# A two-layer encoder on one core: the third branch's attention weights turned by DVE blocks and DRAM transfers in place of TensorE

## The reference, cut to what matters

```python
s = jnp.where(valid, s, -1e30)
lse = jax.nn.logsumexp(s, axis=-1)
o = einsum('bhrnql,bhrnld->bhrnqd', exp(s - lse[..., None]), vb)      # per pattern
...
wts = jax.nn.softmax(jnp.stack(lses, axis=0), axis=0)
o_c = jnp.einsum('gbhs,bhsd->bhsd', wts, outs)
```

## Time and profile before

| | us |
|---|---|
| median of three runs | 1249.8 (1249.55 to 1250.07) |
| the profiled execution's own time | 1250.1 |
| its span, first to last instruction | 1248.1 |
| TensorE busy | 1221.4 (98%) |
| GpSimd busy | 838.0 (67%) |
| DVE busy | 676.7 (54%) |
| ScalarE busy | 433.6 (35%) |
| mean granted TensorE clock, as a share of full speed | 0.997 |

### The profile page before, as it was taken

How to read it: one execution, slowest core, us unless ns; L and a number is a source line. 1 busy time by engine, 2 the same in 40 slices (tenths; PEclk the granted TensorE clock), 3 DMA queues, 4 the chain that set the end, 5 groups by cost and what they waited for, 6 DMA issues and landing times.

```text
span 1248.1 us, 17785 instructions
## 1 busy us (share of the span) xinstructions
PE 1221.4 (98%) x5840; PEld 983.5 (79%) x5840; DVE 676.7 (54%) x1008; ACT 433.6 (35%) x775; POOL 838.0 (67%) x595
## 2 busy tenths in 40 slices
PE   6999999999999999999999999999999999999995
PEld 4887788778878887788888878887887788777884
DVE  5675327522843374677557831573257335738842
ACT  5424423442354245200253453245314532450002
POOL 5597367737763876678849853885498549757871
PEclk9999999999999999999999999999999999999998
DMA  6243223323332333374234332523252315336621
GB/s 240 72 131 121 102 86 117 112 93 101 109 103 93 109 101 118 126 269 151 90 137 143 102 104 77 162 83 107 70 155 87 117 50 151 101 103 228 207 68 67
DMA packets 51794, 148.64 MB, mean 119 GB/s; under 512 B 6560, under 2 KB 8096, under 8 KB 51360
## 3 DMA queue, kind: packets, MB, share of 16 engines
q1 hardware_dynamic: 28800, 103.04, 24.5%
q10 hardware_dynamic: 22944, 44.98, 11.8%
HBM read 114.45 MB, written 16.78 MB: 105 GB/s over the span
## 4 chain that ended last, share of the span: by engine, by line
PE 94%; DVE 3%; POOL 1%; DMA 1%; issue 1%; ACT 0%; POOLq 0%; ACTq 0%; DVEq 0%
PE proj L1047 55%; PE proj L1111 11%; PE turn L1248 4%; PE turn L1177 3%; PE score L1248 3%; PE score L1169 2%; PE mbank L1185 2%; PE score L1170 2%; PE obank L1185 2%; PE mbank L1248 2%; PE obank L1248 2%; PE obank L1199 1%; DMA raw_w<-weights 1%; DVE yl L982 1%; PE score L1137 1%; PE turn L1124 1%
## 5 line engine op out<-in xcount | busy, mean ns | idle before, releaser
L411 POOL TENSOR_TENSOR wl<-raw_w,wh 128x512 fp32r<-128x512 f32 x352 | 510.1, 1469 | 32.3 <-POOL wh L406 32.3
L406 POOL TENSOR_SCALAR wh<-raw_w 128x1024 fp32r<-128x1024 f32 x176 | 215.3, 1223 | 294.1 <-PE proj L1111 137.9
L1047 PE MATMUL proj<-hh,wh 128*128 128x512 f32 x1024 | 405.6, 396 | 0.5 <-DVE big L1009 0.5
L1047 PE MATMUL proj<-hh,wl 128*128 128x512 f32 x1024 | 400.4, 391 | 0.0
L1047 PE MATMUL proj<-hl,wh 128*128 128x512 f32 x1024 | 399.4, 390 | 0.0
L1047 PEld LDWEIGHTS proj<-hh,wl 128*128 128x128 f32 x1024 | 192.2, 188 | 41.6
L1047 PEld LDWEIGHTS proj<-hh,wh 128*128 128x128 f32 x1024 | 192.4, 188 | 40.9 <-issue 1.3
L1047 PEld LDWEIGHTS proj<-hl,wh 128*128 128x128 f32 x1024 | 192.5, 188 | 39.2
L688 ACT ACTIVATE big<-turn 128x512 f32<-128x512 f32 x96 | 56.2, 594 | 88.4 <-PE turn L1177 88.4
L510 ACT ACTIVATE six<-big 128x512 f32<-128x512 f32 x24 | 15.0, 629 | 205.5 <-DVE big L1009 203.7
L902 DVE CUSTOM_DVE_ANT_0 six<-score,lmask 128x512 f32<-128x512 f32 x64 | 43.3, 686 | 79.1 <-PE score L1170 78.8
(11 more groups left out here) (184 smaller groups left out, 1876.8 us busy)
## 6 DMA issues: line engine op xcount, KB each, us to landing
raw_w<-weights SPq DMA_DIRECT2D x175, 512.0 KB, 3.3
gate_scratch<-gstage ACTq DMA_DIRECT2D x48, 256.0 KB, 2.0
six<-gate_scratch ACTq DMA_DIRECT2D x16, 768.0 KB, 5.2
big<-big ACTq DMA_DIRECT2D x64, 128.0 KB, 3.4
yh<-yh ACTq DMA_DIRECT2D x64, 128.0 KB, 2.4
big<-x_t SPq DMA_DIRECT2D x4, 512.0 KB, 6.6
big<-x_t SPq DMA_DIRECT2D x1, 2048.0 KB, 8.9
x_scratch<-big SPq DMA_DIRECT2D x1, 2048.0 KB, 7.3
```

The lines of the kernel that those rows point to most:

```text
L406: pool.tensor_scalar(wh[:, slot, :, :], src, 1.0, 1.0, ALU.mult, ALU.mult).then_inc(pool_high.sem, 1)
L411: ins = pool.tensor_tensor(wl[:, slot, half, :], src[:, half, :], wh[:, slot, half, :].bitcast(F32), ALU.subtract)
L1047: last = pe.matmul(dst, a[:, slot, k, :], b[:, k, :], start=(k == 0 and a is wh and b is hh), stop=(k == KT - 1 and a is wl))
```

## The change

B's units are as before. For C's 8 units a group:

- The scaling by the inverse sum moves from DVE to ScalarE (`scale`), in place in `probs`; DVE only computes the inverse (`inverse`).
- DVE transposes the scaled weights in 32x32 blocks from `probs` to `w` (`turn_32`), with the blocks of one quarter of each 128 keys put side by side.
- SP stores that tile to DRAM (256 KB), waits for it, and loads it back in four parts (64 KB each, runs of 512 B), one for each 32 rows of `wt` or `wt1` (`send`). Stores go through two buffers of `w`; DVE waits for the store before it writes the buffer again.
- SP's issues of the first two units stand before the group's last weight load, those of the others before the next group's loads.
- TensorE waits once for all 32 loads (`back`) before C's values; the value product reads the weights with a stride, in runs of 32 columns.
- With no turnings between, the 29 filling steps of the tail stand as 4, 5 and 20; the 20 come behind the last scores.
- On ScalarE the norm of A and B and gate m4 move behind all scalings; on DVE the normed outputs move behind all turnings.

The diff, without the signals' counts and the new DRAM tensor `turn_scratch` of eight 128x512 tiles:

```diff
@@ -340,6 +345,10 @@
                                      yh[own, q_of(n, head):high_of(n, head) + 1:2, :].bitcast(F32), ALU.subtract)
+        def by_quarter(t):
+            return t.rearrange("p (c k j) -> p k c j", c=4, k=QB)
...
@@ -355,6 +364,21 @@
                     "p (t c) -> p t c", c=P)).then_inc(loaded[slot].sem, 16)
+            def send(G, n):
+                if n < 2 * QB:
+                    sp.wait_ge(*turned_32.at(G, n + 1))
+                    sp.dma_start(turned_d[n, :, :], w[:, n % 2, :]).then_inc(sent[n % 2].sem, 16)
+                if n:
+                    m = n - 1
+                    if m == 0:
+                        sp.wait_ge(*out_done.at(G, 3))
+                        sp.wait_ge(*c_parts.at(G, 1))
+                    sp.wait_ge(*sent[m % 2].at(G, 16 * (m // 2 + 1)))
+                    for c in range(4):
+                        sp.dma_start((wt, wt1)[m % 2][32 * c:32 * c + 32, m // 2, :].rearrange("i (a f) -> i a f", a=4),
+                                     turned_d[m, :, P * c:P * c + P].rearrange("(a i) f -> i a f", a=4)).then_inc(back.sem, 16)
...
@@ -373,8 +397,13 @@
                         last = 4 + j - RAW if j >= RAW else 4 + max(n for n in range(GU) if n % RAW == j) - GU
+                        if j == GU - 1:
+                            for n in range(3):
+                                send(L * NG + i, n)
                         sp.wait_ge(*split_done.at(L, i * GU + (last + 1)))
                         unit(L, i * GU + (4 + j), arrival(4 + j)[0])
+                    for n in range(3, 2 * QB + 1):
+                        send(L * NG + i, n)
                 for row in range(BRANCH_ROW + RAW, ROWS_LAYER):
...
@@ -674,7 +703,9 @@
                         act.wait_ge(*max_ready.at(G, j + 1))
-                        if j >= 4:
+                        if j >= 12:
+                            act.wait_ge(*turned_32.at(G, j - 11))
+                        elif j >= 4:
                             act.wait_ge(*w_ready.at(G, unit_of(j - 4) + 1))
...
@@ -682,11 +713,13 @@
                         act.wait_ge(*turn_done.at(G, u + 1))
-                        if u == 4:
-                            act.wait_ge(*out_done.at(G, 3))
-                        q = (u if u < 4 else (u - 4) // 2) * P
-                        act.activation((wt if u < 4 or u % 2 == 0 else wt1)[:, :, q:q + P], turn[u % 2][:, :].rearrange("p (k q) -> p k q", k=QB),
+                        act.activation(wt[:, :, P * u:P * u + P], turn[u % 2][:, :].rearrange("p (k q) -> p k q", k=QB),
                                        ACT.Copy).then_inc(wt_ready.sem, 1)
+                    def scale(n):
+                        act.wait_ge(*rs_ready.at(G, n + 1))
+                        act.activation(probs[:, n % 4, :], probs[:, n % 4, :], ACT.Copy, scale=rs[:, n + 8:n + 9]).then_inc(scaled.sem, 1)
...
@@ -709,24 +742,21 @@
                     act.activation(sqb[:, :], obank[:, :], ACT.Square).then_inc(sq_done.sem, 1)
-                    for u in range(4, 10):
-                        exp(u + 6)
-                        turned(u)
-                        if u == 5:
+                    for n in range(2 * QB):
+                        scale(n)
+                        if n < 6:
+                            exp(n + 10)
+                        if n == 1:
                             merge_gate(2)
-                            act.wait_ge(*out_done.at(G, 2))
-                            grp.did(act.activation(rr[:, 0, :], mbank[:, :], ACT.Ln, bias=cst[:, 0:1]))
-                            act.wait_ge(*out_done.at(G, 4))
-                            grp.did(act.activation(rr[:, 1, :], obank[:, :], ACT.Ln, bias=cst[:, 0:1]))
-                            grp.last()
-                            act.activation(rr[:, :, :], rr[:, :, :], ACT.Exp, scale=-0.5).then_inc(r_done.sem, 1)
-                        if u == 7:
+                        if n == 5:
                             merge_gate(3)
-                        if u == 9:
-                            merge_gate(4)
-                    turned(10)
-                    turned(11)
+                    act.wait_ge(*out_done.at(G, 2))
+                    grp.did(act.activation(rr[:, 0, :], mbank[:, :], ACT.Ln, bias=cst[:, 0:1]))
+                    act.wait_ge(*out_done.at(G, 4))
+                    grp.did(act.activation(rr[:, 1, :], obank[:, :], ACT.Ln, bias=cst[:, 0:1]))
+                    grp.last()
+                    act.activation(rr[:, :, :], rr[:, :, :], ACT.Exp, scale=-0.5).then_inc(r_done.sem, 1)
+                    merge_gate(4)
                     merge_gate(5)
...
@@ -925,22 +955,27 @@
                             dve.wait_ge(*turn_done.at(G, u - 1))
-                        if u < 4:
-                            a, c = 2 * u, 2 * u + 1
-                            dve.wait_ge(*exp_done.at(G, c + 1))
-                            grp.did(dve.reciprocal(rs[:, a:a + 2], sums[:, a:a + 2]))
-                            grp.last()
-                            grp.did(dve.tensor_scalar(rs[:, c:c + 1], rs[:, c:c + 1], sc[:, 2:3], None, ALU.mult))
-                            grp.did(dve.tensor_scalar(w[:, u % 2, :], probs[:, a % 4, :], rs[:, a:a + 1], None, ALU.mult))
-                            grp.last()
-                            dve.scalar_tensor_tensor(w[:, u % 2, :], probs[:, c % 4, :], rs[:, c:c + 1], w[:, u % 2, :],
-                                                     ALU.mult, ALU.add).then_inc(w_ready.sem, 1)
+                        a, c = 2 * u, 2 * u + 1
+                        dve.wait_ge(*exp_done.at(G, c + 1))
+                        grp.did(dve.reciprocal(rs[:, a:a + 2], sums[:, a:a + 2]))
+                        grp.last()
+                        grp.did(dve.tensor_scalar(rs[:, c:c + 1], rs[:, c:c + 1], sc[:, 2:3], None, ALU.mult))
+                        grp.did(dve.tensor_scalar(w[:, u % 2, :], probs[:, a % 4, :], rs[:, a:a + 1], None, ALU.mult))
+                        grp.last()
+                        dve.scalar_tensor_tensor(w[:, u % 2, :], probs[:, c % 4, :], rs[:, c:c + 1], w[:, u % 2, :],
+                                                 ALU.mult, ALU.add).then_inc(w_ready.sem, 1)
+                    def inverse(n):
+                        dve.wait_ge(*exp_done.at(G, n + 9))
+                        dve.reciprocal(rs[:, n + 8:n + 9], sums[:, n + 8:n + 9]).then_inc(rs_ready.sem, 1)
+                    def turn_32(n):
+                        dve.wait_ge(*scaled.at(G, n + 1))
+                        if n < 2:
+                            dve.wait_ge(*turn_done.at(G, n + 3))
                         else:
-                            j = u + 4
-                            dve.wait_ge(*exp_done.at(G, j + 1))
-                            grp.did(dve.reciprocal(rs[:, j:j + 1], sums[:, j:j + 1]))
-                            grp.last()
-                            dve.tensor_scalar(w[:, u % 2, :], probs[:, j % 4, :], rs[:, j:j + 1], None, ALU.mult).then_inc(w_ready.sem, 1)
+                            dve.wait_ge(*sent[n % 2].at(G, 16 * (n // 2)))
+                        dve.transpose(by_quarter(w[:, n % 2, :]), probs[:, n % 4, :].rearrange("p (k c j) -> p k c j", k=QB, c=4)).then_inc(turned_32.sem, 1)
...
@@ -955,19 +990,20 @@
                             silu(2, "cg")
-                    weights(4)
-                    row_max(10)
-                    dve.wait_ge(*sq_done.at(G, 2))
-                    dve.scalar_tensor_tensor(y[:, NG + i, :], obank[:, :], sc[:, 4:5], sg[:, 1, :], ALU.mult, ALU.mult).then_inc(y_read.sem, 1)
-                    for u in range(5, 12):
-                        weights(u)
-                        if u < 10:
-                            row_max(u + 6)
-                        if u == 8:
-                            dve.wait_ge(*r_done.at(G, 1))
-                            dve.wait_ge(*y_read.at(G, 2))
-                            grp.did(dve.tensor_tensor(y[:, i, :], y[:, i, :], rr[:, 0, :], ALU.mult))
-                            dve.tensor_tensor(y[:, NG + i, :], y[:, NG + i, :], rr[:, 1, :], ALU.mult).then_inc(ab_normed.sem, 1)
+                    for n in range(2 * QB):
+                        inverse(n)
+                        if n:
+                            turn_32(n - 1)
+                        if n < 6:
+                            row_max(n + 10)
+                        if n == 0:
+                            dve.wait_ge(*sq_done.at(G, 2))
+                            dve.scalar_tensor_tensor(y[:, NG + i, :], obank[:, :], sc[:, 4:5], sg[:, 1, :], ALU.mult, ALU.mult).then_inc(y_read.sem, 1)
+                    turn_32(2 * QB - 1)
+                    dve.wait_ge(*r_done.at(G, 1))
+                    dve.wait_ge(*y_read.at(G, 2))
+                    grp.did(dve.tensor_tensor(y[:, i, :], y[:, i, :], rr[:, 0, :], ALU.mult))
+                    dve.tensor_tensor(y[:, NG + i, :], y[:, NG + i, :], rr[:, 1, :], ALU.mult).then_inc(ab_normed.sem, 1)
```

(53 more changed lines are left out.)

## The result

The changed kernel takes 1283.1 us, the median of four runs (1281.15 to 1286.45), against 1249.9 before. The ratio is 1.0264, with a 95% interval of 1.0244 to 1.0283: 33 us slower, where 7 were forecast.

A forecast was written before the change was run, and what follows sets the result against it. TensorE, busy 98% of the span, was taken as the bound. 1250.1 - 29.4 saved + 8 x (4.4 + 0.1) of waiting = 1256.7, said as 1257; own range 1248 to 1268, 8 in 10 1230 to 1287.

The forecast's parts named there:

- What goes from TensorE: Group tail: eight of twelve turnings and late product starts leave TensorE, 3.67 us a group, 29.4 over 8 groups.
- The value products read with a stride: C's last value product reading runs of 32 columns: extra cost taken as nothing, at most 0.9 us of 3.58.
- DVE, ScalarE, the gates: New work beside TensorE: turning 0.69 us, scaling 0.60; maxima in time for the scores by 0.05 to 0.2 us.
- the forecast 384.57: Time in one group's tail when TensorE finishes the 60 filling products and is ready for C's values.
- SP's issue cost: SP queue, 40 issues a group: block load 0.485 us, store 0.66, unit 2.6; called the deciding term.
- Rivals 1 to 3: SP issue cheap or overlapped, 1221 (0.10); in between, 1227 to 1244 (0.22); 0.62 us a block load, 1287 (0.16).
- rival 3: SP queue: a block load costs 0.62 us like the 32-partition copies, 3.8 us more a group, 1287; chance 0.16.
- A store of this size and direction lands after 2.0 ... SP looks for it only a unit later, so it hides: SP queue: the 256 KB store's landing of 2.0 us costs SP no wait; even 2.7 would hide.
- the held-up weight load 0.4: SP queue in the tail: the weight load issued among the stores and loads costs 0.4 us of issue.
- 6.4 were forecast: C's values begin at 389.0 instead of 388.24: 0.8 us more per group, 6.4 in all.
- TensorE waits 4.4 us; with 0.1 to restart: Before C's values: TensorE ready at 384.57, last load landing at 388.9, values beginning at 389.0.
- Rival 4: The wait before C's values makes TensorE's clock fall, some 1.4 us in every group, 11 us: 1268; chance 0.12.

The follow-up runs named there:

- experiment 6: Changed kernel without the stores and loads of the turned weights; the last value product reads cos and sin instead: 1223.3 us, 0.9785.
- experiment 2: Kernel before the change, with only C's value products reading their operand in runs of 32 columns: 1250.7 us, 1.0009.
- Experiment 4: Also `load_first`: changed kernel with the group's last weight load issued before all stores and loads of the turned weights: 1269.3 us, 1.0145.
- experiment 10: Also `act_quarter`: changed kernel, weight load first, ScalarE issuing one of the four loads of units 0 to 5: 1239.2 us, 0.9920.
- experiment 9: Also `paired`: changed kernel, weight load first, 16 loads of 128 KB a group in place of 32 of 64 KB: 1279.1 us, 1.0231.
- contig: Changed kernel with the last value product reading its weights in contiguous runs of 512 columns: 1284.3 us, 1.0272.
- half_bytes: Changed kernel with four loads a unit as before, each of 32 KB, half the weights not loaded: 1274.1 us, 1.0196.
- act_half: Changed kernel, weight load first, ScalarE issuing two of the four loads of units 0 to 5: 1242.3 us, 0.9926.
- warm: Changed kernel with 20 unread products on TensorE between the filling and the wait for the loads: 1269.3 us, 1.0144.
- load_first_warm: Changed kernel with the weight load before all stores and 15 unread products before TensorE's wait: 1255.5 us, 1.0045.

## Why the prediction was wrong

The direction was right and the size was not. By its own steps:

- **What goes from TensorE: right.** 3.67 us a group forecast, 3.62 measured (experiment 6). The value products read with a stride cost nothing, as taken (experiment 2).
- **DVE, ScalarE, the gates: right where it counts.** A turning takes 0.703 us (0.69 taken), a scaling 0.717 (0.60 taken, 0.72 was the upper bound). The last scores, forecast in time by 0.05 to 0.2, are some 0.3 us late in six of the eight groups: the filling ends 27.3 us after B's first value product there, 27.0 in the other two. It costs nothing, since TensorE waits for the loads anyway. The filling ends at 390.94 (395.86 - 4.92), against the forecast 384.57 moved by the 6.21 that this group begins late: 390.78.
- **SP's issue cost: right.** Block loads start 0.47 us apart (0.485 taken), a unit takes 2.4 to 2.5 us (2.6 taken; of this the 0.2 for the store's two waits is 0.15 by the forecast's own 37 ns). Rivals 1 to 3 all fall with this; that rival 3's time (1287) lies near the result is chance, since its spacing of 0.62 is not there. The Trainium skill's sentence, in "DMA: Bandwidth & Descriptors", section "Issuing engines are not separate DMA queues", that the sequencer time saved by a second issuing engine is usually small beside the DMA does not carry over to this list of 64 KB loads: the measurement decides. One issue is 0.47 us against 2.2 to land, but they stand in a row, and six a group moved to ScalarE were worth 30 us (1269.3 to 1239.2), the clock's part included.
- **"A store of this size and direction lands after 2.0 ... SP looks for it only a unit later, so it hides", and "the held-up weight load 0.4": the first failed step.** The 0.4 us is only the weight load's issue. Its 512 KB were issued just ahead of a store, which lands after 4.28 us in place of 2.0 (4.1 to 4.9 in the eight groups). SP looks for it 2.84 us after it began to issue it, which would have hidden 2.7 as forecast, and stands 1.46 us (12.2 in all). C's product begins 32.24 us after B's on average, against 30.64: 1.6 us a group more, 12.8 in all, where 6.4 were forecast. The pauses are more than this difference because the rest of the step was priced too high: a unit 2.6 for 2.4, the last landing 2.7 for 2.45. Experiment 4 takes the pause away (C's product 30.76 us after B's): 14 us. What makes the store slow is shown only so far: the load ahead of it does. Whether by standing in the same queue or by loading the same DMA engines, no run separates; ScalarE's 256 KB stores of `gate_scratch`, in another queue, also land later than before (2.9 us at the median, 2.0 in the earlier trace rows).
- **"TensorE waits 4.4 us; with 0.1 to restart": the second and larger failed step.** The forecast charged the wait at its length and the product behind it at 3.58. The clock fell to 0.50 in every one of the eight waits and the products took 46.3 us, not 28.7: 17.6 us. Rival 4 had this mechanism, and was wrong twice: its chance was put at 0.12, and its price (1.4 us a group, read off the start of the kernel, where only two products ran slowly) was too low. The product behind the wait is sixteen fp32 instructions long, and lost 2.2 us of the 3.58 that half clock throughout would cost (an estimate: its own length once more). The rows pointed there: the earlier trace rows showed a clock that had fallen within 4.5 us of TensorE's last product, and the wait forecast was 4.4. The Trainium skill, in "TensorE: Matmul & The Clock Gate", section "Part 1: The HAM clock gate", has an idle engine fall back to half rate; the runs agree (granted clock 0.50 in each of the eight waits).

The sum: 6.4 forecast + 6.4 for the stores + 17.6 for the clock = 30.4 of the 31.2 us by which the span grew. Of the rest, the stretch between the layers, from the fourth group's C product to the fifth group's B product, is 1.6 us longer (208.2 against 206.6) and the others together 0.8 shorter; no run shows why. The median of the runs is another 2.0 above the profiled execution (1281.15).

## What to carry to other kernels

Price a new wait on TensorE as its length plus what the products behind it lose at half clock; a wait that cannot be avoided is cheaper filled with unread products. Small DMAs are paid in issue time on one queue: first ask whether the issuing engine is what is late. If it is, any issue taken off its list counts, early ones too (experiment 10); if it waits for data, only those behind the last piece of data do (experiment 9). Before a store for whose completion something waits, look for a bulk transfer issued just ahead of it, and move that.

## What the runs showed of the hardware

How long a wait was and whether C's product behind it was slow, by the timelines (full clock: 3.65 us there):

| kernel | waits, us | products |
|---|---|---|
| after | 4.8 to 5.9 | all eight slow, 5.0 to 6.3 |
| `load_first` | 3.2 to 4.5 | all eight slow, 5.1 to 6.4 |
| `contig`, `half_bytes`, `paired` | 3.6 to 6.1 | all slow, 5.0 to 6.6 |
| `act_half` | 1.95, 2.09, 2.80 | slow, 5.1 to 5.4 |
| `act_half` | 1.07 to 2.26, five of them | full speed |
| `warm` | 1.97, 2.53 | slow, 5.35 |
| `warm` | 0.8 to 1.3, six of them | full speed |
| `act_quarter` | 0.83 to 2.83 | full speed |
| `load_first_warm` | up to 1.5, five of them | full speed |

All waits of 3.2 us and more cost the clock, none up to 1.7 did, and in between both happened. Two waits of nearly one length, first from TensorE's timeline of `act_quarter`, then from that of `act_half`:
```profile
742.06 3.65 PE L1228 MATMUL mbank<-big,group 128*64 128x512 f32 x16 [2.83 <-DMA big<-turn_scratch]
```
```profile
386.66 5.14 PE L1228 MATMUL mbank<-big,group 128*64 128x512 f32 x16 [2.80 <-DMA big<-turn_scratch]
```
What decides there stays open. It also shows in the spread of `act_quarter`: the runs with a mean clock of 0.997 took 1234.5 and 1237.3 us, those at 0.992 and 0.993 took 1242.1 and 1241.0.

The completion of a 256 KB store depends on what was issued just ahead of it: 2.0 to 2.2 us at the median, 4.28 behind a 512 KB load, 4.16 behind eight loads of 128 KB and a store. An fp32 moving operand read in runs of 32 columns is free at full clock (598 ns an instruction with and without).
